# Reading the second mixer's wide input weight from contiguous tiles instead of from strided columns

## The reference

```python
h = rmsnorm_2(x, g_mix)
proj = h @ w_in                      # w_in: [1024, 8208] float32
fox_qkv, fox_f, sc_bcv, dn_qkv, dn_b, dn_a, dn_z, br_gate = split_cols(proj, IN_SIZES)
...                                  # forgetting attention, gated short convolution, gated delta rule
gates = jax.nn.sigmoid(br_gate).reshape(bsz, seq, N_BRANCH, D_MODEL)
merged = jnp.sum(jnp.einsum('bsnc,ncd->bsnd', ys, w_branch) * gates, axis=2)
x = x + merged @ w_o
...                                  # convolution MLP, then a gated per-layer embedding
```

## Time and profile before

| | |
|---|---|
| median of 3 timed runs | 1023.29 us (1022.83 to 1025.29) |
| the profiled execution's own time | 1022.01 us |
| span of its trace | 1020.2 us |
| TensorE busy | 964.4 us, 95% |
| VectorE, ScalarE busy | 744.3 us (73%), 501.6 us (49%) |
| moved by DMA | 171.76 MB, 168 GB/s over the span |
| transfers from the two input weights | 46 of 1 MB: 14 of the first mixer, 32 of the second |

### The profile page before, as it was taken

How to read it: one execution, slowest core, us unless ns; L and a number is a source line. 1 busy time by engine, 2 the same in 40 slices (tenths; PEclk the granted TensorE clock), 3 DMA queues, 4 the chain that set the end, 5 groups by cost and what they waited for, 6 DMA issues and landing times.

```text
span 1020.2 us, 17808 instructions
## 1 busy us (share of the span) xinstructions
PE 964.4 (95%) x7576; PEld 904.6 (89%) x7576; DVE 744.3 (73%) x1083; ACT 501.6 (49%) x623; POOL 16.7 (2%) x35
## 2 busy tenths in 40 slices
PE   5999999899989999989998989989999999999997
PEld 3578999898989999988997989989989999999986
DVE  5879988878888798847977966644595776666664
ACT  5644344625464464427754544324543554545463
POOL 0000000002000000000100000000000000000000
PEclk9999999999989999979999999999999999999999
DMA  9997353364366557654756875735653455555541
GB/s 339 284 294 257 115 166 125 124 207 143 114 226 214 193 173 247 174 116 83 145 122 152 139 151 172 123 97 118 143 180 129 145 192 180 195 178 195 176 165 42
DMA packets 142719, 171.76 MB, mean 168 GB/s; under 512 B 3241, under 2 KB 129473, under 8 KB 142641
## 3 DMA queue, kind: packets, MB, share of 16 engines
q1 hardware_dynamic: 140352, 165.63, 55.7%
q0 software_dynamic: 1088, 2.57, 0.7%
q10 hardware_dynamic: 1200, 2.43, 0.7%
HBM read 169.55 MB, written 1.06 MB: 167 GB/s over the span
## 4 chain that ended last, share of the span: by engine, by line
PE 59%; DVE 10%; ACT 4%; issue 3%; DMA 2%; DVEq 0%; ACTq 0%
PE bank L1140 18%; PE bank L1142 17%; PE bank L1141 17%; DVE wlo L604 3%; ACT whi L595 2%; PE bank L1678 2%; DMA raw<-in_w_in_dram 1%; DVE arena L2326 1%; DVE arena L2191 1%; PE bank L1619 1%; DVE arena L2287 1%; DVE arena L1865 1%; DMA raw<-in_w_up_dram 1%; ACT arena L953 0%; PE bank L1455 0%
## 5 line engine op out<-in xcount | busy, mean ns | idle before, releaser
L1140 PE MATMUL bank<-hhi,whi 128*128 128x256 f32 (+1 forms) x1744 | 512.6, 294 | 23.7 <-issue 8.0
L1141 PE MATMUL bank<-hlo,whi 128*128 128x256 f32 (+1 forms) x1744 | 505.4, 290 | 0.0
L1142 PE MATMUL bank<-hhi,wlo 128*128 128x256 f32 (+1 forms) x1744 | 505.3, 290 | 0.0
L604 DVE TENSOR_TENSOR wlo<-raw,whi 128x2048 fp32r<-128x2048 f32 x131 | 299.7, 2290 | 151.2 <-ACT whi L595 110.7
L1140 PEld LDWEIGHTS bank<-hhi,whi 128*128 128x128 f32 x1744 | 339.7, 195 | 33.2 <-issue 21.1
L1141 PEld LDWEIGHTS bank<-hlo,whi 128*128 128x128 f32 x1744 | 340.0, 195 | 4.1 <-issue 1.2
L1142 PEld LDWEIGHTS bank<-hhi,wlo 128*128 128x128 f32 x1744 | 339.6, 195 | 2.5
L595 ACT ACTIVATE whi<-raw 128x2048 fp32r<-128x2048 f32 x131 | 250.5, 1912 | 119.6 <-PE bank L1142 69.1
L1140 PE MATMUL bank<-whi,hhi 128*128 128x256 f32 (+1 forms) x256 | 88.2, 344 | 0.8 <-ACT arena L1102 0.8
L1141 PE MATMUL bank<-wlo,hhi 128*128 128x256 f32 (+1 forms) x256 | 86.7, 339 | 0.0
L1142 PE MATMUL bank<-whi,hlo 128*128 128x256 f32 (+1 forms) x256 | 86.6, 338 | 0.0
(11 more groups left out here) (351 smaller groups left out, 866.9 us busy)
## 6 DMA issues: line engine op xcount, KB each, us to landing
raw<-in_w_in_dram SPq DMA_DIRECT2D x46, 1024.0 KB, 8.4
raw<-in_w_up_dram SPq DMA_DIRECT2D x44, 1024.0 KB, 5.1
raw<-in_w_down_dram SPq DMA_DIRECT2D x22, 1024.0 KB, 5.0
raw<-in_w_ada_dram SPq DMA_DIRECT2D x19, 1024.0 KB, 5.3
raw<-in_w_branch_dram SPq DMA_DIRECT2D x6, 1024.0 KB, 5.4
arena<-in_w_ada_dram SPq DMA_DIRECT2D x10, 512.0 KB, 9.3
raw<-in_w_out_dram SPq DMA_DIRECT2D x4, 1024.0 KB, 5.0
raw<-in_w_o_dram SPq DMA_DIRECT2D x4, 1024.0 KB, 5.1
```

Source lines behind the costliest of these rows:

```text
L604: dve.tensor_tensor(wlo[:, g % RING, :], raw[:, n % RING, :], whi[:, g % RING, :].bitcast(F32), ALU.subtract).then_inc(w_lo, 1)
L1140: pe.matmul(o, wh, ah, start=start, stop=False, **kw)
L1141: pe.matmul(o, wh, al, start=False, stop=False, **kw)
L1142: return pe.matmul(o, wl, ah, start=False, stop=stop, **kw)
```

## The change

The host cuts the second mixer's input weight into 32 tiles of 128 x 2048 floats, one for each chunk, each laid out as `raw` wants it. A partition's 8 pieces now follow one another, 8192 bytes, and the partitions follow one another, so a chunk is 1 MB of contiguous memory. The device reads tile t instead of a strided slice. Order, sizes, buffers, semaphores and arithmetic stay as they are; the narrow columns (`w_small`) were laid out by the host before already.

```diff
+FOX, SC, DN, DN_Z, GATE = 0, 1544, 3080, 4624, 5136
+W_IN2 = (("dq", DN, 2), ("dk", DN + 512, 2), ("dv", DN + 1024, 2), ("fq", FOX, 2), ("fk", FOX + 512, 2),
+         ("fv", FOX + 1024, 2), ("scc", SC + 512, 2), ("scv", SC + 1024, 2), ("scb", SC, 2), ("dz", DN_Z, 2),
+         ("gs", GATE + D, 4), ("gf", GATE, 4), ("gd", GATE + 2 * D, 4))
...
+    w = x["w_in_2"][0]
+    tiles = np.stack([w[:, c:c + 256].reshape(KT, P, 256).transpose(1, 0, 2).reshape(P, CHUNK)
+                      for _, c0, n in W_IN2 for c in range(c0, c0 + 256 * n, 256)])
+    return {"table": table, "w_small": w_small, "w_in2_tiles": tiles}
...
-            chunk(f"{name}{c}", cols(w_in2, c0 + 256 * c), (KT, 256))
+    def in2(name):
+        chunk(name, i["w_in2_tiles"][tile_of[name]].rearrange("p (k n) -> p k n", k=KT), (KT, 256))
...
-            chunk(f"g{name}{c}", cols(w_in2, GATE + D * n + 256 * c), (KT, 256))
+            in2(f"g{name}{c}")
```

More of the change, by code:

```diff
@@ L98, in host_layout @@
         w_small[:, row:row + n] = x["w_in_2"][0][:, c0:c0 + n]
-    return {"table": table, "w_small": w_small}
+    w = x["w_in_2"][0]
+    tiles = np.stack([w[:, c:c + 256].reshape(KT, P, 256).transpose(1, 0, 2).reshape(P, CHUNK)
+                      for _, c0, n in W_IN2 for c in range(c0, c0 + 256 * n, 256)])
+    return {"table": table, "w_small": w_small, "w_in2_tiles": tiles}
 def build(nc, i, out):
@@ L152, in build @@
     ffn_chunks("f", w_up, w_down)
[L153 to L157, removed]
+    w_branch = i["w_branch_2"][0]
+    tile_of = {f"{name}{c}": t for t, (name, c) in enumerate((name, c) for name, _, n in W_IN2 for c in range(n))}
+    def in2(name):
+        chunk(name, i["w_in2_tiles"][tile_of[name]].rearrange("p (k n) -> p k n", k=KT), (KT, 256))
+    for name, _, n in W_IN2[:-3]:
         for c in range(n):
-            chunk(f"{name}{c}", cols(w_in2, c0 + 256 * c), (KT, 256))
+            in2(f"{name}{c}")
     for name, n in (("s", 1), ("f", 0), ("d", 2)):
         for c in range(4):
-            chunk(f"g{name}{c}", cols(w_in2, GATE + D * n + 256 * c), (KT, 256))
+            in2(f"g{name}{c}")
         for c in range(2):
```

## The result

The changed kernel takes 1011.41 us (median of 4 runs, 1010.39 to 1013.22), the one before 1023.06 (4 runs, 1022.70 to 1025.29): a ratio of 0.990, 95% interval 0.986 to 0.994. The profiled execution took 1010.39 us, its span is 1008.6 instead of 1020.2. Lines of the file stand 10 lower after the change, so 595 is now 605, 1678 is 1688.

What follows compares the result with a forecast made beforehand. TensorE bounds the kernel, busy 964.4 of 1020.2 us; only its waits and half clock can go. 1.09 + 2.87 + 1.2 make 5.2, plus 0.5 is 5.7; 1022.0 - 5.7 = 1016.3, plus 1.3 gives 1017.6, range 1013.0 to 1021.8.

Steps and rivals of the forecast that it cites:

- Transfers: Second mixer's input weight: a tile chunk alone lands in 5.0 us, bounds 4.5 and 5.5, 2.9 more when queued.
- the two near 525 us: Transfers of `scc0` and `scc1`, one queued behind the other: as tiles they land within 8 us.
- The 32,832-byte step of the rows, or where a piece starts: Second mixer's weight: what is left as cause of slow transfers, 11.5 us at 520 to 560 us, not piece size.
- The chain behind `scc1`: ACT's split 4.5 us earlier; TensorE's waits of 1.09 and 2.87 us and 1.2 of half clock go: 5.2 us.
- Given back: Line 1586: TensorE waits 1.2 us, its lead falls to 4.5, then returns to 5.2 at line 1604.
- so they don't hold it: Scores: line 2356's reciprocal ends at 560.9 us, TensorE finishes `scv0` at 564.1, so no wait there.
- The clock at line 1604: Wait shrinks from 2.1 to 1.4 us; if the clock stays up about 1 us is gained, half taken, 0.5.
- The gate chunks are late for nobody ... and they gain nothing.: Second mixer's gate chunks: ACT has no wait for them, so tiles for them gain nothing.
- (b): Line 1678: slow gate chunk delays instruction fetching; pause and half clock go too, 4.1 us more, 1013.5; chance 0.17.
- (d): Second mixer: instruction fetches delayed by runs eight times as long, 4.1 us each, three give 1029.9; chance 0.06.

## Why the prediction was wrong

- **Transfers: right.** 5.0 us were taken, 4.9 measured; the two near 525 us took 6.5 and 6.7, within the 8 foretold. That the size of the pieces was not the cause was right as well. "The 32,832-byte step of the rows, or where a piece starts" was half right: it is the step, but no rule of a step near a power of two.
- **The chain behind `scc1`: right.** ACT's split starts at once behind `fv0`, 0.76 us of general lateness apart at the time forecast; both waits are gone, and the clock stays up. 5.2 us were forecast by the end of `scv0`, 5.9 came.
- **Given back: right in size, wrong in place.** A new wait of 1.2 us was expected at line 1586. It came one step earlier, at line 1578 (the scores), for the same reason: DVE's chain was only 4.5 us ahead. The sentence "so they don't hold it" looked at the reciprocal, which did end in time; the scores' last banks are emptied by DVE's line 2379, behind two splits of 4.5 us together.
- **The clock at line 1604: mis-sized.** 0.5 us were taken, 1.7 came in this execution. The pause ahead of it did not shrink (2.1 us, as before), since the lead of 4.5 us was that of DVE too; the clock stayed up all the same. In another execution of the same source it did not, so these 1.7 us are luck of the one execution.
- **The step that failed: "The gate chunks are late for nobody ... and they gain nothing."** It was read from ACT's waits, which are for data. TensorE waited for its own instructions, and what held them up was a gate chunk. This was rival (b), with a price of 4.1 us; measured are 4.9 and 5.8. I gave it 0.17 since "nothing in the rows ties the two". The queues' view would have: no instruction packet in the 10.5 us of `gf3`'s transfer, one just at its end. With (b) taken in, the sum would have been 5.7 + 4.1, 1013.5, and the remaining 2 us are mostly clock, of which the second MLP's first chunks have 1.5.
- **(d), slower through instruction fetches behind long runs**: fetches do wait for a tile's transfer to be nearly through (4.5 us of `gf3`'s 4.9), but not so long that TensorE feels it. It is the length in time of the transfer that counts, 1024-byte runs or not.

## What to carry to other kernels

A transfer whose data nobody waits for can still cost time: instruction fetches use the same DMA engines, so where TensorE stops inside a row of equal instructions with "issue" as the reason, look at which transfer is in flight and when the instruction queue's packets come. When one weight lands slower than others of the same piece size, try another row length before laying out tiles: 64 bytes less in each row, with the 16 narrow columns left out, gave the whole gain here. Tile only what is slow: tiles for weights that landed in 5.1 to 5.5 us brought the kernel no time, and at its head they came with later first transfers.

## What the runs showed of the hardware

- Rows of 32,832 bytes: medians of 8.8 to 11.9 us for 1 MB in 1024-byte pieces; of 32,768, 33,024, 36,864 and 36,928 bytes: 5.0 to 5.8. The Trainium skill ("DMA: Bandwidth & Descriptors", section "Latency and other measured facts") warns of pitches at large powers of two, 512 KB and up; here the power of two itself, 32 KB, was fast, and 64 bytes more was slow.
- TensorE's instructions come over the same 16 DMA engines as the data, 16 KB at a time. The same fetch started 4.5 us into a transfer of 4.9 us and 10.7 us into one of 11.4, and TensorE, out of instructions by then, went on 2.3 us later.
- With the slow layout a kernel's runs spread over 9 us (1016.4 to 1025.7 in 31 runs), the changed kernel's over 3 us or less in two times 4. A slow transfer's length goes with the place and the kernel (`gf3`: 11.2 to 14.5 us over four kernels, 14.2 and 14.5 in two executions of one), and the solver's pause with the start of the fetch (3.6 and 5.4 us in those two). How much of the 9 us that makes is not shown.
- The same pause of 2.1 us at the products of the values is followed by half clock in some executions (4.2 to 4.5 us for the 32 products) and by full clock in others (2.8 us), also between two executions of one and the same kernel. What decides it is open. It is worth 1.7 us a time, as much as a small change to the kernel.
